# Pattern A's score matmuls: one fp32 product becomes two fp32r products of split operands

## The chip, the cores and the metric

One Trainium2 chip, and the kernel runs on one of its cores. The metric is the device time of one execution in microseconds. "Before" was run three times, beside one execution under the profiler.

## What is computed

A two-layer encoder trunk. In each layer the normalised input (512 tokens, 1024 features) goes through one wide projection, four attention patterns read parts of it, each pattern's output is projected, gated and summed, and an MLP follows. The change is in pattern A, a windowed attention with 8 query heads on 2 key/value heads:

```python
def windowed_gqa(a_q, a_k, a_v, pos, q_norm, k_norm, sink):
    q = rms_norm(a_q.reshape(b, s, A_KV_HEADS, grp, HEAD_DIM), q_norm)   # 8 heads of 64
    k = rms_norm(a_k.reshape(b, s, A_KV_HEADS, HEAD_DIM), k_norm)        # 2 heads of 64
    ...
    o, _ = banded_attention(q, k, v, pos, A_RADIUS, slopes, sink)        # |i - j| <= 128
# banded_attention: s = q.k / sqrt(d) - slope*|pos_i - pos_j|, masked outside the band,
# softmax with the sink logit in the denominator, then p.v
```

## The kernel before

**Two sorts of matmul.** The projections use split operands: a float32 value x is stored as a high part (x rounded to the type fp32r) and a low part (x minus the high part, also fp32r), and a product is three fp32r matmuls, high by high, low by high, high by low (`split3`; the matmuls all carry line L565). Weights arrive in `s_raw`, ACT writes the high part `s_wh` (L937), DVE the low part `s_wl` (L1413). The attention's transposes (L594), its values (L787) and its scores (L797, for pattern B L841) are matmuls of plain float32 operands instead. The profile has two LDWEIGHTS and two MATMUL instructions for each float32 score or value matmul, and one of each for a fp32r one.

**An order written out by hand.** A layer is 752 steps; a step is the six L565 matmuls of two chunks for one of the four output banks. `ORDER` lays the projections on the steps. Every other piece of work is a generator that yields the step at which it is due (`yield at`), and `together` merges the generators of an engine by due time into its one instruction stream, which the engine then runs strictly in that order, each instruction behind its semaphore waits. So a wait on an engine holds all that stands behind it. A weight tile's split (L937, L1413) is due 7.6 steps before the tile's first use, if its buffer is free.

**Attention.** `WINDOW` gives each pattern its stretch of steps; pattern A has steps 312 to 376 and 32 units (one head of one tile of 128 queries each, 8 heads for a tile) on 36 slots, one slot each 1.78 steps. In a slot PE transposes the probabilities of unit u-2 (L594), multiplies those of unit u-3 with the values (L787), and makes the scores of unit u into the bank S1 (L797). A unit has 256 key columns in tiles 0 and 3 and 384 in tiles 1 and 2 (`near_keys`). PE makes the scores of unit u only after `s_biased` of unit u-1: DVE adds the bias to S1 (L1918), ACT takes the exponential (L1236, L1241), ACT and DVE each copy half of the transposes (L1229, L1854).

**The queries of A.** `qA` has two heads in the two halves of the partitions. ACT copies them to `q_pad` [128, 4, 2, 128], where a head stands in its own 64 partitions and the other 64 are zero, so that one matmul over 128 partitions with `kA` (both halves hold the same key head) gives that head's scores. `tiles_of` does this in 8 pieces of two copies (L1270), four heads of one tile in a piece; a piece is due almost a whole piece of units ahead of its first unit, except the first two, which are due half a step before slot 0. PE waits for `q_padded` before a unit's scores. `kA` is written by ACT at L1182 behind the "kv" projection, in four turns; in the same turns ACT and DVE write the latent's high (L1185) and low (L1795) parts, and PE's next turn waits for them on `td_act` and `td_dve`.

Of the kernel before, what the change touches and what calls it, by code (L numbers as in the profile page):

```python
# [13 lines left out]
F32 = mybir.dt.float32  # L14
# [92 lines left out]
class Own:  # L107
# [13 lines left out]
    nt_dve=24, ta_ready=128, ta_act=128, ta_dve=128, q_padded=64, s_ready=144, s_biased=144, p_ready=144, b_mixed=16, o_ready=128, o_out=24,  # L121
    gains_in=1, ssum=16, lam_dot=1, lam_exp=1, c_diff=2, c_exp=2, merged_sum=24, merged_hi=8, merged_lo=8, conv_mid=44,
    e_ready=22, hidden_val=22, hidden_hi=22, hidden_lo=22, act_step=189, dve_step=513, params_in=16, direct_in=8,
# [41 lines left out]
PADS = dict(C0=16, C1=8, C2=8, A=16, B=16)  # L165


def pads_of(name, u):

    return u + 1 if PADS[name] == 8 else 4 * (u // 8) + 2 * (u % 8 // 4) + 2  # L170

# [53 lines left out]
def _build(nc, io, ctx):  # L225
# [23 lines left out]
    AD = 7168  # L249
    work = sb("work", [P, AD + 15872])  # L250
# [31 lines left out]
    kA, vA = in_work(AD + 14336, 1024, g=2), in_work(AD + 15360, 512, t=4)  # L282
# [54 lines left out]
    q_padded = signal("q_padded")  # L337
    s_ready = signal("s_ready")
# [191 lines left out]
    def _(pe):  # L530
# [3 lines left out]
        def layer(l):  # L534
# [227 lines left out]
            def attention(name, scores_of, values_of, per_out, begun, keys=all_keys, tile_of=None):  # L762
# [6 lines left out]
                for step, at, pace in slots(name):  # L769
# [19 lines left out]
                    if step < n:  # L789
                        if step == 0:  # L790
                            for handle, count in begun:
                                pe.wait_ge(handle, count)
                        if name in PADS:
                            pe.wait_ge(*q_padded.at(l, pads + pads_of(name, step)))
                        pe.wait_ge(*s_biased.at(l, first + step))
                        for out, st, mv in scores_of(step, S1):
                            last = mm(out, st, mv, start=True, stop=True)  # L797
                        last.then_inc(*s_ready.up())
# [9 lines left out]
            def attention_b(scores_of, begun):  # L808
# [5 lines left out]
                for step, at, pace in slots("B"):  # L814
# [19 lines left out]
                    if step < n:  # L834
                        if step == 0:
                            for handle, count in begun:
                                pe.wait_ge(handle, count)
                        pe.wait_ge(*q_padded.at(l, n_pad[0] + pads_of("B", step)))
                        pe.wait_ge(*s_biased.at(l, first + step))
                        for out, st, mv in scores_of(step, S1):  # L840
                            mm(out, st, mv, start=True, stop=True).then_inc(*s_ready.up())  # L841
# [11 lines left out]
            def attentions():  # L853

                def near_scores(k_of):
                    def scores_of(u, out):
                        lo, hi, _mid = near_keys(u)
                        h = u % 8
                        return [(out[:, P * lo:P * hi], q_pad[:, h // 2, h % 2, :], k_of(h)[:, P * lo:P * hi])]
                    return scores_of  # L860

                def residue_scores(j):
                    return lambda h, out: [(out[:, P * r:P * r + P], q_pad[:, r, h % 2, :],
                                            CK[j][:, h // 2, P * r:P * r + P]) for r in range(RES)]
# [5 lines left out]
                def b_scores(u, out):  # L870
                    n = 4 * (u % 2) + (u % 8) // 2
                    return [(out[:], q_pad[:, n // 2, n % 2, :], kT[:, n // 2, :])]
# [7 lines left out]
                for j in (1, 2):  # L880
                    yield from attention(f"C{j}", residue_scores(j), residue_values(j), 2, heads_in(8 * j + 9, 12 * j + 12))
                yield from attention("D", lambda u, out: [(out[:], qD[0:DQK, u % 8, P * (u // 8):P * (u // 8) + P], kD[0:DQK, u % 8, :])],
                                     token_values(lambda u, k: vD[u % 8 // 4][:, k, DV * (u % 4):DV * (u % 4) + DV], DV, 8), 8,
                                     heads_in(53, 68), tile_of=out_tiles)
# [11 lines left out]
    def _(act):  # L896
# [47 lines left out]
        def layer(l):  # L944
# [304 lines left out]
            def pads():  # L1249
# [21 lines left out]

                def residues_of(j, turns_done):
# [18 lines left out]
                yield from tiles_of("A", qA, 57, by_pair)  # L1291
# [60 lines left out]
    def _(dve):  # L1352
# [62 lines left out]
        def layer(l):  # L1415
# [356 lines left out]
            def turns():  # L1772
# [189 lines left out]
            return norm1(), dense(), turns(), attentions(), c_combine()  # L1962
# [31 lines left out]
```

## Time and profile before

| | |
|---|---|
| three runs | 2741.24, 2744.35, 2745.07 us; median 2744.35 us |
| the profiled execution | 2741.32 us; its span, first to last instruction, 2739.5 us |
| mean granted TensorE clock | 0.996 of full speed |
| busy | PE 97%, weight loads 81%, DVE 57%, ACT 45% of the span |

The span is what the trace shows; 1.8 us of the profiled execution lie around it. The profile names the engines PE (matmuls), PEld (their weight loads), DVE (VectorE), ACT (ScalarE) and SP (SyncE). L and a number is a line of the kernel. A tile's name is that of its memory: `s_work` holds nearly all the attention tiles. The trace calls the type of fp32r matmul operands f32; an L565 matmul is fp32r.

### The profile page before, as it was taken

What the parts mean: (1) busy time and instruction counts of PE and PEld (TensorE: products, weight loads), DVE (VectorE), ACT (ScalarE), POOL (GpSimd) and SP (SyncE); (2) the same over time, 40 slices, a digit from 0 to 9 for tenths busy, and PEclk for the clock granted to TensorE, in tenths of its full rate; (3) what the DMA queues carried; (4) which work ended last, traced back from release to release, by engine and by line L of the source; (5) the groups of instructions that cost most, each with busy time, mean ns of one, the idle gap of its engine ahead of it and who ended that gap; (6) DMA issues with size and microseconds to landing.
All of it is one profiled execution on the core that took longest, in us unless ns stands there. A gap on an engine that the chain in (4) does not pass through costs nothing. (4 is left out here: it accounts for less than half of the span.)

```text
span 2739.5 us, 35859 instructions
## 1 busy us (share of the span) xinstructions
PE 2644.2 (97%) x12974; PEld 2215.0 (81%) x12974; DVE 1565.9 (57%) x3276; ACT 1232.0 (45%) x2510; POOL 1.5 (0%) x6
## 2 busy tenths in 40 slices
PE   5999999999999989999999999999999999899999
PEld 4899987777877778888879998877788777788887
DVE  5564577544566556464764546775455566464645
ACT  5455555444544334242454555544445443342423
POOL 0000000000000000000000000000000000000000
PEclk9999999999999999999999999999999999999999
DMA  5212223222121323333342122221222213232333
GB/s 167 77 55 78 81 63 92 62 65 82 55 72 52 101 86 92 100 93 100 93 123 70 47 86 74 80 83 54 70 78 68 63 47 108 85 100 93 99 93 100
DMA packets 143872, 225.26 MB, mean 82 GB/s; under 512 B 15046, under 2 KB 69458, under 8 KB 142802
## 3 DMA queue, kind: packets, MB, share of 16 engines
q1 hardware_dynamic: 135842, 201.85, 24.7%
q10 hardware_dynamic: 7856, 21.12, 2.1%
q8 instruction: 106, 1.74, 0.3%
q14 instruction: 68, 0.56, 0.1%
HBM read 210.29 MB, written 12.65 MB: 81 GB/s over the span
## 5 line engine op out<-in xcount | busy, mean ns | idle before, releaser
L1413 DVE TENSOR_TENSOR s_wl<-s_raw,s_wh 128x1024 fp32r<-128x1024 f32 (+2 forms) x376 | 453.7, 1207 | 382.0 <-ACT s_wh L937 380.6
L937 ACT ACTIVATE s_wh<-s_raw 128x1024 fp32r<-128x1024 f32 (+2 forms) x376 | 392.3, 1043 | 440.8 <-PE bank L565 423.3
L565 PE MATMUL bank<-s_hTh,s_wh 128*128 128x512 f32 x1216 | 520.4, 428 | 3.6 <-DVE s_hTl L1517 3.6
L565 PE MATMUL bank<-s_hTh,s_wl 128*128 128x512 f32 x1216 | 474.7, 390 | 0.0
L565 PE MATMUL bank<-s_hTl,s_wh 128*128 128x512 f32 x1216 | 473.9, 390 | 0.0
L565 PE MATMUL bank<-s_wh,s_hTh 128*128 128x512 f32 (+1 forms) x1088 | 469.6, 432 | 3.5 <-DVE s_early L1530 3.3
L565 PE MATMUL bank<-s_wh,s_hTl 128*128 128x512 f32 (+1 forms) x1088 | 426.0, 392 | 0.0
L565 PE MATMUL bank<-s_wl,s_hTh 128*128 128x512 f32 (+1 forms) x1088 | 425.4, 391 | 0.0
L565 PEld LDWEIGHTS bank<-s_hTh,s_wh 128*128 128x128 f32 x1216 | 228.6, 188 | 70.9 <-issue 27.3
L1241 ACT ACTIVATE s_work<-s_work,s_stat 128x128 f32<-128x128 f32 (+3 forms) x320 | 167.5, 524 | 257.7 <-DVE s_work L1929 113.5
L565 PEld LDWEIGHTS bank<-s_hTl,s_wh 128*128 128x128 f32 x1216 | 228.8, 188 | 66.6 <-issue 24.4
L565 PEld LDWEIGHTS bank<-s_wh,s_hTh 128*128 128x128 f32 x1088 | 251.8, 231 | 37.5 <-issue 3.7
L565 PEld LDWEIGHTS bank<-s_wl,s_hTh 128*128 128x128 f32 x1088 | 253.5, 233 | 27.4 <-issue 0.5
L565 PEld LDWEIGHTS bank<-s_wh,s_hTl 128*128 128x128 f32 x1088 | 251.6, 231 | 26.9
L565 PEld LDWEIGHTS bank<-s_hTh,s_wl 128*128 128x128 f32 x1216 | 228.2, 188 | 49.0
L594 PE MATMUL bank<-s_consts,s_work 128*128 128x128 f32 (+1 forms) x1432 | 216.3, 273 | 11.6 <-DVE s_gTl L1770 7.3
L594 PEld LDWEIGHTS bank<-s_consts,s_work 128*128 128x128 f32 (+1 forms) x1432 | 173.1, 139 | 65.0 <-issue 28.2
L1854 DVE COPY s_work<-bank 128x128 f32<-128x128 f32 (+1 forms) x224 | 77.5, 346 | 230.4 <-PE bank L594 111.8
L565 PE MATMUL bank<-s_wh,s_gTh 128*128 128x512 f32 (+1 forms) x432 | 167.6, 388 | 5.3 <-ACT s_work L965 5.3
L565 PE MATMUL bank<-s_wh,s_gTl 128*128 128x512 f32 (+1 forms) x432 | 166.9, 386 | 0.0
L565 PE MATMUL bank<-s_wl,s_gTh 128*128 128x512 f32 (+1 forms) x432 | 166.8, 386 | 0.0
L1229 ACT ACTIVATE s_work<-bank 128x256 f32<-128x256 f32 (+1 forms) x224 | 78.4, 350 | 92.8 <-PE bank L594 91.3
(189 smaller groups left out, 3376.9 us busy)
## 6 DMA issues: line engine op xcount, KB each, us to landing
s_raw<-in_w_in SPq DMA_DIRECT2D x168, 512.0 KB, 3.6
s_raw<-in_ffn_w_up SPq DMA_DIRECT2D x176, 256.0 KB, 3.1
s_raw<-in_ffn_w_down SPq DMA_DIRECT2D x44, 512.0 KB, 3.7
s_raw<-in_w_branch SPq DMA_DIRECT2D x32, 512.0 KB, 3.7
s_raw<-in_w_o SPq DMA_DIRECT2D x16, 512.0 KB, 3.7
x_keep<-s_work ACTq DMA_DIRECT2D x2, 2048.0 KB, 6.9
s_raw<-in_w_in SPq DMA_DIRECT2D x16, 256.0 KB, 2.9
gate_keep<-s_early ACTq DMA_DIRECT2D x4, 1024.0 KB, 4.3
```

Of the source, the lines that this page charges most:

```text
L565: last = mm(PJ[b][:, 0:width], st, mv, start=i == 0 and n == 1, stop=i == ntiles - 1 and n == 3 * chunks)
L594: last = nc.tensor.transpose(dst[0:m, (at + n) * P:(at + n) * P + k], src, ident[0:k, 0:k])
L937: a(wh[:, k % 3, 0:n], raw[:, s, 0:n], ACT.Copy).then_inc(*hi_split.up(own))
L1229: a(probsT[:, u % 2, P * lo:P * mid], src[:, P * lo:P * mid], ACT.Copy).then_inc(*ta_act.up(own))
L1241: a(probs[:, u % 2, x0:x0 + w], scores[:, u % 2, x0:x0 + w], ACT.Exp, scale=-1.0, bias=stat[:, mins, c:c + 1], accum_out=stat[:, sums, c:c ...
L1413: v.tensor_tensor(wl[:, k % 3, 0:n], raw[:, k % 2, 0:n], wh[:, k % 3, 0:n].bitcast(F32), ALU.subtract).then_inc(*tile_split.up(own))
L1854: v.tensor_copy(probsT[:, u % 2, P * mid:P * hi], src[:, P * mid:P * hi]).then_inc(*ta_dve.up(own))
```

## The change

- `kA` becomes fp32r. ACT writes the high part in all 128 partitions as before (L1182), and DVE then overwrites partitions 64 to 127 with the low part: four new DVE instructions a layer, one in each turn of "kv", ahead of L1795's.
- The queries of A go to `q_two` [128, 4 pairs, 2 halves, 2 sets, 128], fp32r, in a part of `s_work` that pattern D's keys leave free. Set 0 is the head's high part, in both halves of the partitions; set 1 is its low part in partitions 0 to 63 and zero below.
- ACT writes the high part once (16 copies of 64x256 a layer, in place of the 16 to `q_pad`) and, ahead of the first piece, the zeros (two copies of 64x512). DVE writes the second copy of the high part from the first, across the partitions, and subtracts to make the low part: two instructions for each of ACT's 16, in a new stream `stacks()` due 0.1 step behind ACT's.
- PE makes a unit's scores with two fp32r matmuls that accumulate: set 0 with `kA` (high query by high key, plus high query by low key in the other half) and set 1 with `kA` (low query by high key). It waits for `q_stacked` in place of `q_padded`, and at slot 0 also for `q_zeroed`.
- All other lines of the diff only pass `start` and `stop` along.

```diff
-PADS = dict(C0=16, C1=8, C2=8, A=16, B=16)
+PADS = dict(C0=16, C1=8, C2=8, B=16)
...
+    kA, vA = stacked[:, AD + 14336:AD + 15360].rearrange("p (g n) -> p g n", g=2), in_work(AD + 15360, 512, t=4)
+    q_two = stacked[:, AD + 4096:AD + 6144].rearrange("p (c h s n) -> p c h s n", c=4, h=2, s=2)
...
+                        if name == "A":
+                            pe.wait_ge(*q_stacked.at(l, pads_of(name, step)))
...
+                def stacked_scores(u, out):
+                    lo, hi, _mid = near_keys(u)
+                    h = u % 8
+                    return [(out[:, P * lo:P * hi], q_two[:, h // 2, h % 2, s, :],
+                             kA[:, h // 4, P * lo:P * hi], s == 0, s == 1) for s in range(2)]
...
-                yield from attention("A", near_scores(lambda h: kA[:, h // 4, :]),
+                yield from attention("A", stacked_scores,
...
-                                     heads_in(57, 72), keys=near_keys, tile_of=out_tiles)
+                                     heads_in(57, 72) + [q_zeroed.at(l, 2)], keys=near_keys, tile_of=out_tiles)
...
+                def stacks_of_a():
+                    first, slot = done, slots("A")
+                    for piece in range(8):
+                        t, g = piece // 2, piece % 2
+                        yield slot[4 * piece - 4][1] + 0.8 * slot[0][2] if piece >= 2 else slot[0][1] - 0.5
+                        if piece == 0:
+                            act.wait_ge(*td_dve.at(l, 57))
+                        act.wait_ge(*s_ready.at(l, first + 4 * piece - 4 if piece >= 2 else first))
+                        if piece == 0:
+                            for half in range(2):
+                                act.wait_ge(*own.done(l))
+                                a(q_two[64:128, :, half, 1, :], q_pad[64:128, :, 0, :], ACT.Copy).then_inc(*q_zeroed.up(own))
+                        for half in range(2):
+                            mine = slice(64 * half, 64 * half + 64)
+                            act.wait_ge(*own.done(l))
+                            a(q_two[mine, 2 * g:2 * g + 2, half, 0, :], qA[mine, 2 * g:2 * g + 2, P * t:P * t + P],
+                              ACT.Copy).then_inc(*q_hi.up(own))
...
                 for t in range(4):
                     yield END["kv"] + 6.8 + 2 * t
                     src = group()
+                    key = kA[64:128, :, P * t:P * t + P]
+                    dve.wait_ge(*own.done(l))
+                    v.scalar_tensor_tensor(key, src[64:128, 0:256].rearrange("p (c n) -> p c n", c=2), prm[64:128, ROW["ak"]:ROW["ak"] + 1],
+                                           key.bitcast(F32), ALU.mult, ALU.subtract).then_inc(*dve_step.up(own))
...
+            def stacks():
+
+                slot, n = slots("A"), 0
+                for piece in range(8):
+                    t, g = piece // 2, piece % 2
+                    yield (slot[4 * piece - 4][1] + 0.8 * slot[0][2] if piece >= 2 else slot[0][1] - 0.5) + 0.1
+                    for half in range(2):
+                        n += 1
+                        mine, other = slice(64 * half, 64 * half + 64), slice(64 - 64 * half, 128 - 64 * half)
+                        dve.wait_ge(*q_hi.at(l, n))
+                        dve.wait_ge(*own.done(l))
+                        v.tensor_copy(q_two[other, 2 * g:2 * g + 2, half, 0, :], q_two[mine, 2 * g:2 * g + 2, half, 0, :].bitcast(F32)).then_inc(*dve_step.up(own))
+                        dve.wait_ge(*own.done(l))
+                        v.tensor_tensor(q_two[0:64, 2 * g:2 * g + 2, half, 1, :], qA[mine, 2 * g:2 * g + 2, P * t:P * t + P],
+                                        q_two[mine, 2 * g:2 * g + 2, half, 0, :].bitcast(F32), ALU.subtract).then_inc(*q_stacked.up(own))
...
-            return norm1(), dense(), turns(), attentions(), c_combine()
+            return norm1(), dense(), turns(), stacks(), attentions(), c_combine()
```

## Rows read from the trace of the kernel before

**Rows 1.** The page's first part: busy time, share, instructions by engine.

```profile
PE 2644.2 (97%) x12974; PEld 2215.0 (81%) x12974; DVE 1565.9 (57%) x3276; ACT 1232.0 (45%) x2510; POOL 1.5 (0%) x6
```

**Rows 2.** Windows over pattern A, layer 0: us, busy by engine, clock, DMA share, GB/s.

```profile
653.00:715.00 62.00, 61.27 (x317) 50.16 (x316) 32.74 (x75) 29.67 (x80) 0.00 (x0) 1.00 0.26 77
715.00:777.00 62.00, 60.89 (x338) 50.94 (x336) 40.77 (x109) 36.34 (x99) 0.00 (x0) 1.00 0.25 75
```

**Rows 3.** PE's waits: total us, times, longest.

```profile
PE bank L797 <- DVE s_stat L1918: 1.5, 2, 0.7
...
PE bank L594 <- DVE s_gTl L1795: 1.0, 2, 0.5
```

**Rows 4.** Timeline, a 256-column unit: start us, us, engine, line, operands, idle before.

```profile
661.79 0.56 PE L787 MATMUL bank<-s_work 128*128 128x64 f32 x4
...
662.18 0.65 PE L797 MATMUL bank<-s_work,s_q_pad 128*128 128x256 f32 x2
...
662.48 0.58 PE L565 MATMUL bank<-s_gTh,s_wh 128*128 128x512 f32 x1
```

**Rows 5.** Timeline, a 384-column unit.

```profile
701.03 0.78 PE L787 MATMUL bank<-s_work 128*128 128x64 f32 x6
...
701.65 0.86 PE L797 MATMUL bank<-s_work,s_q_pad 128*128 128x384 f32 x2
```

**Rows 6.** Timeline, fp32r matmuls of 384 columns: first and eleventh in a row.

```profile
402.00 0.33 PE L565 MATMUL bank<-s_wh,s_gTh 128*128 128x384 f32 x1
...
403.75 0.33 PE L565 MATMUL bank<-s_wl,s_gTh 128*128 128x384 f32 x1
```

**Rows 7.** Groups by shape, ACT and DVE: busy us, mean ns of one, idle before.

```profile
L1284 ACT ACTIVATE s_q_pad<-s_work 64x512 f32<-64x512 f32 x16 | 10.1, 630 | 1.5
...
L1369 DVE CAST s_work<-s_work 128x512 f32<-128x512 int32 x1 | 0.4, 427 | 0.0
...
L1548 DVE TENSOR_TENSOR s_work<-s_work,s_trig 128x256 f32<-128x256 f32 x4 | 1.7, 426 | 0.1
...
L1505 DVE SCALAR_TENSOR_TENSOR s_hTl<-bank,s_prm,s_hTh 128x256 fp32r<-128x256 f32 x32 | 15.3, 483 | 14.4 <-ACT s_hTh L1027 13.1
```

**Rows 8.** Timeline, slots 0 and 1 of pattern A in layer 0.

```profile
651.35 1.82 ACT L1270 ACTIVATE s_q_pad<-s_work 64x256 f32<-64x256 f32 x4
...
653.16 0.59 PE L797 MATMUL bank<-s_work,s_q_pad 128*128 128x256 f32 x2
...
653.98 0.48 DVE L1918 CUSTOM_DVE_ANT_0 s_work<-bank,s_near,s_sink 128x256 f32<-128x256 f32 x1 [3.42 <-PE bank L797]
...
654.98 0.59 PE L797 MATMUL bank<-s_work,s_q_pad 128*128 128x256 f32 x2
```

**Rows 9.** Timeline, piece 2 of the queries and what follows it.

```profile
670.11 0.86 ACT L1270 ACTIVATE s_q_pad<-s_work 64x256 f32<-64x256 f32 x2
...
671.36 0.29 DVE L1854 COPY s_work<-bank 128x128 f32<-128x128 f32 x1 [1.79 <-ACT s_work L1229]
...
672.70 0.48 DVE L1918 CUSTOM_DVE_ANT_0 s_work<-bank,s_near,s_sink 128x256 f32<-128x256 f32 x1
...
673.33 0.67 PE L797 MATMUL bank<-s_work,s_q_pad 128*128 128x256 f32 x2 [0.73 <-DVE s_stat L1918]
```

**Rows 10.** Timeline, piece 4 of the queries and DVE's next instruction.

```profile
700.28 0.86 ACT L1270 ACTIVATE s_q_pad<-s_work 64x256 f32<-64x256 f32 x2
...
701.70 0.29 DVE L1854 COPY s_work<-bank 128x128 f32<-128x128 f32 x1 [2.44 <-PE bank L594]
```

**Rows 11.** Timeline, the first two turns of "kv" and PE's next turns.

```profile
365.39 0.74 DVE L1795 SCALAR_TENSOR_TENSOR s_gTl<-bank,s_prm,s_gTh 128x128 fp32r<-128x128 f32 x2
...
366.28 1.06 PE L594 MATMUL bank<-s_consts,s_work 128*128 128x128 f32 x8
...
370.12 0.74 DVE L1795 SCALAR_TENSOR_TENSOR s_gTl<-bank,s_prm,s_gTh 128x128 fp32r<-128x128 f32 x2 [1.84 <-ACT s_gTh L1185]
...
371.00 0.63 PE L594 MATMUL bank<-s_consts,s_work 128*128 128x128 f32 x4 [0.49 <-DVE s_gTl L1795]
```

More of the change, by code:

```diff
@@ L120 @@
     pj_dve=108, sq_used=60, normed=53, combined=4, sublayer_normed=4, h_normed=5, h_scaled=3, rstd=3, td_ready=77, td_act=77, td_dve=77, nt_ready=16, nt_act=24,
[L121 removed]
+    nt_dve=24, ta_ready=128, ta_act=128, ta_dve=128, q_padded=48, q_hi=16, q_stacked=16, q_zeroed=2, s_ready=144, s_biased=144, p_ready=144, b_mixed=16, o_ready=128, o_out=24,
     gains_in=1, ssum=16, lam_dot=1, lam_exp=1, c_diff=2, c_exp=2, merged_sum=24, merged_hi=8, merged_lo=8, conv_mid=44,
[L123 removed]
+    e_ready=22, hidden_val=22, hidden_hi=22, hidden_lo=22, act_step=189, dve_step=533, params_in=16, direct_in=8,
     x_moved=2, c0_moved=6, gates_moved=4,
@@ L249, in _build @@
     AD = 7168
+    with nc.sbuf_tensor("s_stacked", [P, AD + 15872], F32R) as stacked:
+        pass
     work = sb("work", [P, AD + 15872])
@@ L337, in _build @@
     q_padded = signal("q_padded")
+    q_hi = signal("q_hi")
+    q_stacked = signal("q_stacked")
+    q_zeroed = signal("q_zeroed")
     s_ready = signal("s_ready")
@@ L794, in attention @@
                             pe.wait_ge(*q_padded.at(l, pads + pads_of(name, step)))
+                        if name == "A":
+                            pe.wait_ge(*q_stacked.at(l, pads_of(name, step)))
                         pe.wait_ge(*s_biased.at(l, first + step))
-                        for out, st, mv in scores_of(step, S1):
-                            last = mm(out, st, mv, start=True, stop=True)
+                        for out, st, mv, start, stop in scores_of(step, S1):
+                            last = mm(out, st, mv, start=start, stop=stop)
                         last.then_inc(*s_ready.up())
@@ L839, in attention_b @@
                         pe.wait_ge(*s_biased.at(l, first + step))
-                        for out, st, mv in scores_of(step, S1):
-                            mm(out, st, mv, start=True, stop=True).then_inc(*s_ready.up())
+                        for out, st, mv, start, stop in scores_of(step, S1):
+                            mm(out, st, mv, start=start, stop=stop).then_inc(*s_ready.up())
             def token_values(v_of, width, places, keys=all_keys):
@@ L858, in scores_of @@
                         h = u % 8
-                        return [(out[:, P * lo:P * hi], q_pad[:, h // 2, h % 2, :], k_of(h)[:, P * lo:P * hi])]
+                        return [(out[:, P * lo:P * hi], q_pad[:, h // 2, h % 2, :], k_of(h)[:, P * lo:P * hi], True, True)]
                     return scores_of
+                def stacked_scores(u, out):
[3 more added lines that the diff above has]
+                             kA[:, h // 4, P * lo:P * hi], s == 0, s == 1) for s in range(2)]
                 def residue_scores(j):
                     return lambda h, out: [(out[:, P * r:P * r + P], q_pad[:, r, h % 2, :],
-                                            CK[j][:, h // 2, P * r:P * r + P]) for r in range(RES)]
+                                            CK[j][:, h // 2, P * r:P * r + P], True, True) for r in range(RES)]
                 def residue_values(j):
@@ L871, in b_scores @@
                     n = 4 * (u % 2) + (u % 8) // 2
-                    return [(out[:], q_pad[:, n // 2, n % 2, :], kT[:, n // 2, :])]
+                    return [(out[:], q_pad[:, n // 2, n % 2, :], kT[:, n // 2, :], True, True)]
                 def heads_in(turns_done, evacuated):
@@ L1290, in pads @@
                 done += WINDOW["D"][2]
-                yield from tiles_of("A", qA, 57, by_pair)
+                yield from stacks_of_a()
+                done += WINDOW["A"][2]
                 yield from tiles_of("B", qT, B_HEADS, by_map)
```

5 lines of the change are left out of this document (2 added, 3 removed).

## The prediction

> **What bounds the kernel now.** I read the page's busy line first: PE is busy 97% of the span, DVE 57%, ACT 45% [rows 1]. Busy PE is not PE at its peak, so I next cut out pattern A's window. Its 124 us in layer 0 have 122.2 us of PE at full granted clock, 73.5 us of DVE and 66.0 us of ACT [rows 2]. So PE sets the time there, and a matmul that gets shorter should shorten the kernel, unless PE then waits for another engine. PE's waits say how near that is: once in each layer it waits 0.7 us for DVE's bias before a score, and once in each layer 0.5 us for the low part of the latent in a turn of "kv" [rows 3]. Both places matter below, since the change puts more work on DVE right before them.
>
> **What the scores cost PE now.** Busy times of pipelined matmuls overlap, so I take ends. At a 256-column unit the values end at 661.79+0.56 = 662.35 and the two score instructions at 662.18+0.65 = 662.83: 0.48 us. The next L565 ends at 663.06, 0.23 later, its usual pitch, so nothing of the unit hides beyond its own end [rows 4]. At 384 columns the same difference is 702.51-701.81 = 0.70 us [rows 5]. The 128 columns more cost 0.22 us, 1.7 ns a column: four streams of the columns at 2.4 GHz (0.42 ns each), with about 0.055 us left over that do not grow with the columns.
>
> **What they will cost.** Fp32r streams the columns once. Eleven fp32r matmuls of 384 columns start 1.75 us apart over ten steps, 0.175 each [rows 6]; with 512 columns the pitch is 0.23 [rows 4]. That is 0.42 ns a column and about 15 ns fixed, so 0.121 us at 256 columns, a width for which the trace has no fp32r row. Two of them and the same 0.055 left over: 0.30 us at 256, 0.405 at 384. A unit saves 0.18 or 0.30 us. There are 32 units of each width in the two layers: 5.8 + 9.6 = **15.4 us saved**. Bounds: at 256 columns no faster than the 384 row gives 12.2; with nothing left over beside the two streams it is 18.9.
>
> The Trainium skill's page "TensorE: Matmul & The Clock Gate", section "Back-to-back issue gap", puts a matmul at N/2.4 + 2.5 ns, 109 ns at 256 columns and 163 at 384. By it, and with no remainder, the saving would be 20.7 us. The trace disagrees at 384 columns, where it has 175, so I stay with the rows.
>
> **What DVE gets.** In `stacks()` 16 copies and 16 subtractions a layer, each 256 elements on 64 partitions. The subtraction is like L1548, 0.43 us [rows 7]. For a copy from SBUF to SBUF the nearest row is the CAST of 512 elements in 0.43; half the elements should take 0.28 to 0.30, and never more than the 0.43 of the two-source row. I take 0.29, since CAST is also one source with a change of type. Add some 0.035 between two dependent DVE instructions, an estimate from ACT's own four copies in rows 8, pitched 0.47 at 0.42 long. A half is 0.79 us and **a piece of four 1.58 us**. The four low parts of the keys are like L1505, 0.48 [rows 7]. All this is 8 x 1.58 + 4 x 0.52 = 14.7 us of DVE a layer, 12.6 of them in a window with 50 us of DVE idle. It fits as a sum; what counts is where it falls, as DVE runs in a fixed order.
>
> The page "VectorE: DVE Perf Modes", section "Mode 2×_2P — use both read ports for one tensor", lets a one-source fp32 instruction between SBUF operands make two elements a cycle. The CAST row agrees (512 elements in less time than one a cycle at 0.96 GHz would need). If the copies were refused it, at 0.43 a piece would be 1.86 us, and the forecast some 1.6 us later.
>
> **The start of pattern A.** This is the new wait. Now ACT writes four copies from 651.35 in 1.82 us and PE has its first score at 653.16, without a wait [rows 8]. After: ACT first writes two zero copies of 0.63 (L1284's shape [rows 7]), pitched 0.67, to 652.69, then high part one until 653.10 and two until 653.56. DVE copies and subtracts the first from 653.14 to 653.90 and the second from 653.93 to 654.69. PE's `q_stacked` wait is met at about 654.75: 1.6 us late. Nothing hides this, since all of PE's matmuls stand behind the waiting score. DVE then has piece 1, which is due at the same step, until 656.27, and only then L1918 for unit 0 (now at 653.98), done near 656.8. PE reaches score 1 after 1.6 us of dense work, at 656.35, and waits 0.5 more. Behind DVE's blocks also stands the weights' low part L1413, behind ACT's zeros the high part L937 and one gate's evacuation; these come 1.4 to 2 us later, but a tile is split 7.6 steps (over 10 us) before its use, and the evacuated bank is needed only three steps later, so they stay hidden. Loss **2.1 us a layer**, bounds 1.2 (piece 1 finds a gap) and 3.
>
> **Pieces 2 to 7.** Each is written a slot or more ahead of need, so `q_stacked` is never the late one; the question is whom 1.58 us of DVE push back. Piece 2: ACT's copies start at 670.11, so DVE's block runs 670.56 to 672.14 where it was idle for 1.79 us, but L1854 was due at 671.36 and now starts at 672.17; 1.34 us behind it comes L1918, 673.5 in place of 672.70. PE already waits 0.73 us for that one [rows 9]. So PE loses 0.8 more, and of the savings of the slot before 0.2 are only waited away: 1.0 us. Piece 4: copies from 700.28, DVE's block 700.75 to 702.3, L1854 0.6 late from 701.70, DVE idle 2.44 us before it [rows 10], and L1918 waits for PE's score anyway: nothing. Pieces 3, 5, 6 and 7 I followed in the same way: 3 and 6 push L1918 back by 0.3 and 1.4 us, which is done more than a microsecond before PE's next score; 5 and 7 fall in idle DVE time. **1.0 us a layer**, bounds 0.4 and one more piece exposed (2.6).
>
> **"kv".** The low part of the key delays L1795's end by 0.52 us. In the first turn L1795 ends at 366.13 and PE's next turn starts at 366.28; in the second the ends are 370.86 and 371.00, with 0.49 us of wait already [rows 11]. Both pass on nearly all: **0.9 us a layer**, bounds 0.5 and 1.1. Turns three and four have slack.
>
> **What costs nothing.** ACT's 16 copies keep their number and shape. PE's instruction count stays (two loads and two matmuls a unit), as do the waits.
>
> **The sum.** 2 x (2.1 + 1.0 + 0.9) = 8.0 us lost, 15.4 saved: 7.4 us faster. The profiled execution's 2741.32 would become 2733.9. It lies 3.0 us under the median of the three runs, near the lowest of them; carried over to the median, 2744.35 - 7.4 = **2737 us**.
>
> **The rivals.** 0.2% of this kernel, 5.5 us, is about what a measurement can tell from no change.
> - *As forecast*, 4 to 11 us saved: 0.55, of it 0.43 beyond 5.5 us.
> - *The losses are mostly hidden*: DVE catches up at piece 2, and the start costs only its 1.2 us. Then 15.4 - 2 x (1.2 + 0 + 0.5) = 12.0 saved, 2732.4. For it: four tenths of DVE's time in the window are free [rows 2]. Against: the start's chain has no work over it. 0.20.
> - *PE is handed from matmul to DVE*: two more pieces a layer stand ahead of a bias that PE waits for. 2 x 2 x 1.58 = 6.3 more lost, 1.1 saved, 2743.3. For it: shorter scores bring PE to each wait sooner, and the second half of the window has DVE at 66% [rows 2]. Against: the gaps found at pieces 4, 5 and 7. 0.17.
> - *Slower*: every one of the six later pieces lands ahead of a bias that PE is waiting for. 2 x (2.1 + 6 x 1.58 + 0.9) = 25.0 lost, 9.6 us slower, 2754. It turns the sign from three pieces a layer fully exposed, and passes 5.5 us at 4.7 of six. Against: rows 10. That fp32r at 256 columns streamed more than once is, I think, excluded by the slope between 384 and 512. 0.08.
>
> **How the numbers follow.** Faster 0.43 + 0.20 = 0.63; same 0.12 + 0.17 = 0.29; slower 0.08. The range from 2730 to 2745 takes in the hidden case with the upper bounds of the saving, and the third case; outside are the slower case and an end of the second. The likeliest case's own range is 2733.5 to 2740.5.
>
> **What would show it.** L797 of pattern A as fp32r ends 0.30 and 0.40 us behind the values (0.48 and 0.70 now). DVE has 36 more instructions a layer; the copies near 0.29. A new PE wait of about 1.6 us at the first score of A, another of 0.5 before the second, 1.5 in place of 0.73 at the score behind piece 2 (673.33), and about 0.5 and 1.0 us in "kv". The prediction is wrong if DVE's copies are twice as long, if pieces 3 or 6 show up as PE waits, or if ACT reaches the zeros earlier than 651.35 and takes the start's wait away.

## The result: slower, where 7 us less were forecast

| | median, us | range | runs |
|---|---|---|---|
| before | 2744.27 | 2740.29 to 2746.70 | 20 |
| after | 2748.44 | 2744.83 to 2750.08 | 20 |

The ratio is 1.0016, with a 95% interval of 1.0009 to 1.0023: some 4 us slower, and 3.4 us beyond the upper end of the forecast's range. By the forecast's own bound of 0.2% it counts as no change; the sign is clear all the same. The profiled execution of after took 2744.83 us, its span is 2743.0 against 2739.5, and its mean granted clock 0.994 against 0.996.

The page's first part for after, to lay beside [rows 1]: PE has 10.5 us less to do in the same 12,974 matmuls, DVE 24.3 us more in 72 more instructions.

```profile
PE 2633.7 (96%) x12974; PEld 2211.1 (81%) x12974; DVE 1590.2 (58%) x3348; ACT 1232.7 (45%) x2514; POOL 1.5 (0%) x6
```

Windows over pattern A of layer 0 after (columns as in [rows 2]). PE was busy 122.2 of 124 us; now it is busy 115.3 of 122.0, so about 6.7 us stand open. DVE went from 73.5 us of 124 to 82.9 of 122.

```profile
656.00:718.00 62.00, 58.30 (x318) 49.36 (x319) 39.48 (x95) 30.42 (x83) 0.00 (x0) 1.00 0.26 77
718.00:778.00 60.00, 56.95 (x334) 49.05 (x333) 43.46 (x119) 35.26 (x98) 0.00 (x0) 1.00 0.25 75
```

In after's numbering PE's transposes are L600, its values L793 and its scores L805; the bias is L1971, the halves of the transposes' copies L1243 (ACT) and L1907 (DVE), a tile's output L2000 to L2004. PE's waits of after in the same window (total us, times, longest). Before, the same view has two rows: 0.7 us for the bias, and 1.1 us of L787 for the tile output of L1951.

```profile
PE bank L793 <- DVE s_work L2004: 2.1, 2, 1.5
PE bank L805 <- DVE s_stacked L1886: 1.6, 1, 1.6
PE bank L600 <- DVE s_work L1907: 1.3, 2, 0.9
PE bank L793 <- ACT s_work L1243: 1.1, 1, 1.1
PE bank L805 <- DVE s_stat L1971: 1.1, 2, 0.9
```

**Where the time went.** Both kernels issue the same matmuls in the same order, so I set the profiles side by side matmul by matmul and noted where the difference of their end times, after minus before, jumps by 0.3 us or more. Layer 0:

```
place (time before -> after)               step, us
kv turn 2                 366.28 -> 366.69   +0.53
kv turn 3                 371.00 -> 371.93   +0.52
turn of the next projection
                          391.36 -> 392.81   +0.52
first score of A          653.16 -> 657.09   +1.82
second score                                 +0.27
transposes at piece 2     671.80 -> 676.21   +0.86
values behind piece 3     691.76 -> 695.72   +0.83
values behind tile 1      725.99 -> 728.02   +0.39
transposes at piece 6     739.86 -> 741.52   +0.58
values behind piece 7     761.25 -> 763.03   +1.28
between these, a unit of A          -0.2 or -0.3 each
```

Layer 1 has the same places, with 1.64 at the last. In the window of A the saving wins by 1.25 us in layer 0 and 0.9 in layer 1; "kv" and the turn behind it take 1.57 a layer back. That leaves after some 1.0 us behind. The rest of the 3.5 us between the two profiles comes in two places, in each of which PE runs at half its clock for 3.4 us longer than before: the difference grows by 0.6 us between 410 and 427, and by 2.0 us between 1010 and 1025.

**The saving is there.** Timeline of after, PE, a unit of 256 columns and one of 384 (columns as in [rows 4]). The ends lie 666.51 - 666.23 = 0.28 and 692.04 - 691.63 = 0.41 us apart, 0.48 and 0.70 before.

```profile
665.67 0.56 PE L793 MATMUL bank<-s_work 128*128 128x64 f32 x4
666.03 0.48 PE L805 MATMUL bank<-s_stacked 128*128 128x256 f32 x2
...
691.07 0.56 PE L793 MATMUL bank<-s_work 128*128 128x64 f32 x4
691.44 0.60 PE L805 MATMUL bank<-s_stacked 128*128 128x384 f32 x2
```

Over all units the trace's finer times give 0.291 and 0.403, against 0.488 and 0.701: 32 x 0.197 + 32 x 0.298 = 15.8 us saved. The second matmul of a pair takes 118 ns at 256 columns and 174 at 384. The Trainium skill's page "TensorE: Matmul & The Clock Gate", section "Back-to-back issue gap", would have 109 and 163; the trace lies 9 to 11 ns above them. The remainder that does not grow with the columns stays 55 ns (0.291 less two times 0.118).

**The start of A**, timeline of after. ACT's four copies come behind the zeros, from 654.80; DVE's two halves for piece 0 end at 656.84, and PE waits 1.62 us. DVE then has piece 1's two before the bias at 658.56, for which PE waits 0.27.

```profile
655.25 0.29 DVE L1884 CAST s_stacked<-s_stacked 64x256 fp32r<-64x256 f32 x1 [2.55 <-ACT s_stacked L1301]
655.57 0.42 DVE L1886 TENSOR_TENSOR s_stacked<-s_work,s_stacked 64x256 fp32r<-64x256 f32 x1
...
657.09 0.47 PE L805 MATMUL bank<-s_stacked 128*128 128x256 f32 x2 [1.62 <-DVE s_stacked L1886]
...
658.56 0.48 DVE L1971 CUSTOM_DVE_ANT_0 s_work<-bank,s_near,s_sink 128x256 f32<-128x256 f32 x1
...
659.20 0.48 PE L805 MATMUL bank<-s_stacked 128*128 128x256 f32 x2 [0.27 <-DVE s_stat L1971]
```

**Piece 2**, the counterpart of [rows 9]. DVE's block pushes its half of the transposes' copies (L1907) back, and PE now waits 0.89 us at the next transposes and 0.86 at the score.

```profile
674.28 0.29 DVE L1884 CAST s_stacked<-s_stacked 64x256 fp32r<-64x256 f32 x1 [0.99 <-ACT s_stacked L1301]
...
675.79 0.28 DVE L1907 COPY s_work<-bank 128x128 f32<-128x128 f32 x1
...
676.21 0.41 PE L600 MATMUL bank<-s_consts,s_work 128*128 128x128 f32 x2 [0.89 <-DVE s_work L1907]
...
677.87 0.47 PE L805 MATMUL bank<-s_stacked 128*128 128x256 f32 x2 [0.86 <-DVE s_stat L1971]
```

**Behind piece 3**: DVE from the end of the piece to the tile output. The bias of 690.52 is soon enough, as forecast. But DVE then works for 5 us with no gap over 0.2 us, and piece 3's 1.7 us have pushed back everything up to L2004, the output of tile 0, and that is what PE's next values wait for.

```profile
689.86 0.42 DVE L1886 TENSOR_TENSOR s_stacked<-s_work,s_stacked 64x256 fp32r<-64x256 f32 x1
...
690.52 0.62 DVE L1971 CUSTOM_DVE_ANT_0 s_work<-bank,s_near,s_sink 128x384 f32<-128x384 f32 x1
...
691.06 0.68 DVE L1563 SCALAR_TENSOR_TENSOR s_work<-s_work,bank 128x512 f32<-128x512 f32 x1
...
692.38 1.22 DVE L1446 TENSOR_TENSOR s_wl<-s_raw,s_wh 128x1024 fp32r<-128x1024 f32 x1
...
693.52 0.28 DVE L1907 COPY s_work<-bank 128x128 f32<-128x128 f32 x1
...
693.72 0.61 DVE L1971 CUSTOM_DVE_ANT_0 s_work<-bank,s_near,s_sink 128x384 f32<-128x384 f32 x1
...
694.88 0.69 DVE L2004 TENSOR_TENSOR s_work<-bank,s_stat 128x512 f32<-128x512 f32 x1
```

**"kv"**, the counterpart of [rows 11], and the turn of the projection behind it, whose low part (L1838) ends DVE's chain.

```profile
366.69 1.06 PE L600 MATMUL bank<-s_consts,s_work 128*128 128x128 f32 x8 [0.68 <-DVE s_gTl L1832]
...
371.93 0.63 PE L600 MATMUL bank<-s_consts,s_work 128*128 128x128 f32 x4 [1.00 <-DVE s_gTl L1832]
...
392.81 0.52 PE L600 MATMUL bank<-s_consts,s_work 128*128 128x128 f32 x3 [0.60 <-DVE s_gTl L1838]
```

**DVE's new instructions**, groups by shape. The durations are as forecast; a half takes 0.84 us from start to start, a piece of four 1.68.

```profile
L1886 DVE TENSOR_TENSOR s_stacked<-s_work,s_stacked 64x256 fp32r<-64x256 f32 x32 | 13.4, 419 | 1.1
L1884 DVE CAST s_stacked<-s_stacked 64x256 fp32r<-64x256 f32 x32 | 9.2, 288 | 17.0 <-ACT s_stacked L1301 14.7
L1828 DVE SCALAR_TENSOR_TENSOR s_stacked<-bank,s_prm,s_stacked 64x256 fp32r<-64x256 f32 x8 | 3.9, 491 | 9.2 <-ACT s_gTh L1199 9.0
```

### The profile page after: what moved, and what is told of

It reads as the page before. It is cut to its first block and busy times, and to the rows that moved or that the text cites. A ratio compares the mean times of both kernels' runs of the same rounds, so it can differ in the third digit from the quotient of the medians.

```text
span 2743.0 us, 35969 instructions
## 1 busy us (share of the span) xinstructions
PE 2633.7 (96%) x12974; PEld 2211.1 (81%) x12974; DVE 1590.2 (58%) x3348; ACT 1232.7 (45%) x2514; POOL 1.5 (0%) x6
## 5 line engine op out<-in xcount | busy, mean ns | idle before, releaser
L571 PE MATMUL bank<-s_wh,s_hTh 128*128 128x512 f32 (+1 forms) x1088 | 457.4, 420 | 3.6 <-DVE s_early L1563 3.3
L600 PE MATMUL bank<-s_consts,s_work 128*128 128x128 f32 (+1 forms) x1432 | 216.3, 273 | 16.9 <-DVE s_gTl L1803 6.8
L600 PEld LDWEIGHTS bank<-s_consts,s_work 128*128 128x128 f32 (+1 forms) x1432 | 173.1, 139 | 70.9 <-issue 33.7
L1907 DVE COPY s_work<-bank 128x128 f32<-128x128 f32 (+1 forms) x224 | 77.3, 345 | 204.4 <-PE bank L600 96.5
L1243 ACT ACTIVATE s_work<-bank 128x256 f32<-128x256 f32 (+1 forms) x224 | 78.0, 348 | 85.9 <-PE bank L600 84.7
```

The costliest lines, as they stand in the source:

```text
L571: last = mm(PJ[b][:, 0:width], st, mv, start=i == 0 and n == 1, stop=i == ntiles - 1 and n == 3 * chunks)
L600: last = nc.tensor.transpose(dst[0:m, (at + n) * P:(at + n) * P + k], src, ident[0:k, 0:k])
L1243: a(probsT[:, u % 2, P * lo:P * mid], src[:, P * lo:P * mid], ACT.Copy).then_inc(*ta_act.up(own))
L1907: v.tensor_copy(probsT[:, u % 2, P * mid:P * hi], src[:, P * mid:P * hi]).then_inc(*ta_dve.up(own))
```

## The experiments

Twelve kernels were measured in three sets, each set beside its own runs of the kernel before (median 2743.20, 2743.37 and 2743.49 us). "To before" is the difference of medians. The mean clock is TensorE's granted clock, 1 being full speed. All but `keycost` start from the kernel after.

| kernel | median, us | runs | to before | ratio, 95% | mean clock |
|---|---|---|---|---|---|
| again | 2748.29 | 11 | +4.9 | 1.0009 to 1.0026 | 0.9929 |
| nostack | 2733.08 | 5 | -10.1 | 0.9950 to 0.9975 | 0.9942 |
| nokey | 2741.87 | 11 | -1.3 | 0.9986 to 1.0004 | 0.9943 |
| early | 2742.31 | 11 | -0.9 | 0.9992 to 1.0010 | 0.9935 |
| actcopy | 2754.41 | 5 | +11.2 | 1.0026 to 1.0051 | 0.9920 |
| matmulonly | 2729.38 | 5 | -14.0 | 0.9941 to 0.9966 | 0.9948 |
| halves | 2742.99 | 11 | -0.4 | 0.9991 to 1.0009 | 0.9939 |
| placed | 2742.70 | 11 | -0.7 | 0.9989 to 1.0007 | 0.9936 |
| nocopy | 2739.07 | 11 | -4.4 | 0.9974 to 0.9991 | 0.9939 |
| pool | 2735.00 | 6 | -8.5 | 0.9959 to 0.9982 | 0.9935 |
| poolkv | 2732.69 | 5 | -10.8 | 0.9948 to 0.9973 | 0.9940 |
| keycost | 2747.99 | 11 | +4.5 | 1.0008 to 1.0026 | 0.9943 |

The kernel before has a mean clock of 0.9945 to 0.9947 over the 70 runs beside them. The intervals reach some 2.4 us to either side with 11 runs and 3.4 us with 5 or 6, so differences under 3.5 us between two of these rows are not read.

**nostack: the scores without DVE's stacks.** Both score matmuls read ACT's high part; DVE's copies and subtractions are gone, the keys' low parts stay.

```diff
-            return norm1(), dense(), turns(), stacks(), attentions(), c_combine()
+            return norm1(), dense(), turns(), attentions(), c_combine()
...
-                            a(q_two[mine, 2 * g:2 * g + 2, half, 0, :], qA[mine, 2 * g:2 * g + 2, P * t:P * t + P],
+                            a(q_two[:, 2 * g:2 * g + 2, half, 0, :], qA[:, 2 * g:2 * g + 2, P * t:P * t + P],
```

> The changed kernel without DVE's stream of copies and subtractions: ACT writes the high parts of both heads over all 128 partitions (same count and length of ACT copies), both score matmuls use set 0, and PE waits for ACT alone. Left out: the queries' low parts and the separation of the two heads. PE's two fp32r matmuls, the zeros and the keys' low part stay. Theory 1 (DVE's blocks stand ahead of DVE work for which PE waits; by lining up the two profiles matmul by matmul they cost 12.4 us, the saving 15.8): some 11 us below the changed kernel, 2737. Theory 2 (the saving is lost to a lower granted clock and not to DVE's blocks): within 3 us of the changed kernel, above 2745. Theory 3 (the fp32r matmuls save less than the pitch says): not below 2741.

Measured -10.1 us to before, 2733, where the first theory said 2737. It is the one that fits: the other two needed 2741 or more. The 64 instructions of the stacks cost 15 us in the kernel after, nearly all of the saving, though their 22.6 busy us have 100 us of idle DVE time in the two windows. Of the 15 us, the higher clock (0.9942 for 0.9929 in `again`) makes up to 3.6.

**nokey: without the keys' low part.**

```diff
-                    v.scalar_tensor_tensor(key, src[64:128, 0:256].rearrange("p (c n) -> p c n", c=2), prm[64:128, ROW["ak"]:ROW["ak"] + 1],
-                                           key.bitcast(F32), ALU.mult, ALU.subtract).then_inc(*dve_step.up(own))
```

> The changed kernel without the four DVE instructions a layer that write the keys' low part (left out: that part; the lower half of the keys keeps the high part). Theory 1: PE's turns of kv and of cq come 1.45 us a layer earlier, so 2.9 us below the changed kernel, about 2745.5. A rival, that these waits are absorbed by later ones: no difference.

Measured 6.2 us less than `again`, each against its own before, twice what was expected. The forecast gave these eight instructions 1.8 us; 2 x 1.57 = 3.1 are the waits seen above, and the clock (0.9943 for 0.9929) is worth up to 3.8.

**early: pieces 0 and 1 six steps sooner**, on ACT and DVE, nothing else changed.

```diff
-                        yield slot[4 * piece - 4][1] + 0.8 * slot[0][2] if piece >= 2 else slot[0][1] - 0.5
+                        yield slot[4 * piece - 4][1] + 0.8 * slot[0][2] if piece >= 2 else slot[0][1] - 6.5
```

> The changed kernel with the zeros and pieces 0 and 1 due six steps earlier, at step 305.5 on ACT and 305.6 on DVE, behind the last scores of pattern D. Theory 1: PE's wait before the first scores of A goes (1.8 and 0.3 us in each layer), so 4.2 us below the changed kernel, about 2744.3. Rival: DVE's block now falls before D's tile outputs and PE waits there instead: no gain.

Measured 5.8 us less than `again`, against twice the forecast start of 2.1 = 4.2; the clock (0.9935 for 0.9929) is worth up to 1.6. PE's waits in its window (640 to 780): those of the start are gone, all others stand, and one of 0.3 us is new.

```profile
PE bank L793 <- DVE s_work L2004: 2.1, 2, 1.5
PE bank L600 <- DVE s_work L1907: 1.3, 2, 0.9
PE bank L793 <- ACT s_work L1243: 1.2, 1, 1.2
PE bank L805 <- DVE s_stat L1971: 0.9, 1, 0.9
PE bank L793 <- DVE s_work L1907: 0.3, 1, 0.3
```

**actcopy: ACT makes the second copy instead of DVE.**

```diff
                             a(q_two[mine, 2 * g:2 * g + 2, half, 0, :], qA[mine, 2 * g:2 * g + 2, P * t:P * t + P],
+                              ACT.Copy).then_inc(*act_step.up(own))
+                            other = slice(64 - 64 * half, 128 - 64 * half)
+                            act.wait_ge(*own.done(l))
+                            a(q_two[other, 2 * g:2 * g + 2, half, 0, :], qA[mine, 2 * g:2 * g + 2, P * t:P * t + P],
                               ACT.Copy).then_inc(*q_hi.up(own))
...
-                        v.tensor_copy(q_two[other, 2 * g:2 * g + 2, half, 0, :], q_two[mine, 2 * g:2 * g + 2, half, 0, :].bitcast(F32)).then_inc(*dve_step.up(own))
```

> The changed kernel with ACT writing both copies of the high half (32 ACT copies a layer for 16), DVE only the subtraction. DVE's piece falls from 1.68 to about 0.9 us, ACT's grows from 0.9 to 1.8. Theory 1: pieces 2 to 7 cost half of 8.2 us, the start costs the same or 0.3 more a layer: 3 to 4 us below the changed kernel, about 2745. Theory 4 (in this window ACT is as tight as DVE): no gain or a loss, with new PE waits for ACT's L1243 and for the banks' evacuation.

Measured +11.2 us to before, 6 us worse than the kernel after, where the first theory said 3 to 4 us better; the fourth came true. ACT is 45% busy over the span and has no room here either, since it makes the exponentials and half of the copies that hand PE its probabilities. In the window of A of layer 0, PE's waits sum to 8.8 us in place of 7.2: for ACT's copy (L1243) 1.8 in place of 1.1, and for the tile output 2.5 in place of 2.1, though DVE has less to do. The clock, the lowest of all, is worth up to 2.5 us.

**again and matmulonly: the whole cost of DVE's work in one pair.** `again` is the kernel after unchanged; `matmulonly` is `nostack` and `nokey` together, so PE, ACT's copies and the zeros are all that is left of the change.

> The changed kernel as it is, for its time and granted clock beside the others on one chip. Every theory: ratio 1.0016 to before, about 2748; by the amended theory 1 a mean granted clock about 0.001 under that of before (0.9931 to 0.9945 so far), worth some 3 us, and about 1 us of waits over savings.

> The changed kernel without DVE's stacks and without the keys' low part (both left out, as in the two runs before): only PE's two fp32r matmuls in place of the fp32 one, with ACT's zeros. Theory 1: the whole saving of 15.8 us less some 1.2 us for ACT's zeros at the start of A: 14.6 below before, about 2729, with the clock of before (0.9945). Theory 3 (the fp32r matmuls save less): above 2733.

`matmulonly` is 14.0 us under before, which fits the forecast's 15.4 for the matmuls (ACT's zeros still cost a wait of 0.45 us a layer). Matmul by matmul, `again` minus `matmulonly` in layer 0:

```
kv and the projection behind it    0.52  0.54  0.54
start of A                         1.20  0.50
transposes and score at piece 2    0.95
values at tile output 0 (piece 3)  0.72
values behind tile 1               0.24
transposes at piece 6              0.61
values behind piece 7              1.04
```

Layer 1 has the same steps (1.37 behind piece 7). Together 6.9 and 7.2 us of waits. The two kernels are 18.9 us apart; the clock, 0.9948 and 0.9929 of the span, makes up to 5.2 of it. The two, 14.1 and 5.2, add up to the difference within 0.4.

**halves and placed: the pieces spread out.** `halves` is `early` with every piece from the third on cut in two, a slot apart, and due 0.4 of a slot behind its slot's start in place of 0.8. `placed` also gives "kv"'s turns 2.5 steps in place of 2, on PE, ACT and DVE.

```diff
+                            if half and piece >= 2:
+                                yield slot[4 * piece - 4 + 1][1] + 0.4 * slot[0][2]
...
-                    yield END["kv"] + 6.8 + 2 * t
+                    yield END["kv"] + 6.8 + 2.5 * t
```

> The changed kernel with pieces 0 and 1 six steps early (as in the run early) and each later piece in two halves, due in two neighbouring slots and in the middle of the slot (0.4) where it was 0.8. All of DVE's work stays. Theory 1 (what costs is where DVE's blocks stand): the eight us of pieces 2 to 7 fall to two or three, so 4.2 + 5 us below the changed kernel, about 2739. Rival (what costs is the sum of DVE's work): as the run early, 2742 to 2744.

> As halves, and the four turns of kv 2.5 steps apart on PE, ACT and DVE where they were 2. Theory 1: PE's three waits of 0.5 us a layer behind the keys' low parts go as well, 3 us below halves, about 2736, with the clock of before. Rival: the later turns push on those of cq and on DVE's rsqrt, no gain over halves.

Both missed: neither differs from `early`. Matmul by matmul, `halves` gains 0.6 us at piece 2 and 0.6 at piece 6 and loses 0.9 at 688 and 0.95 around 692, where the half-pieces of piece 3 now stand before the transposes' copies and the tile output. The waits move and keep their sum, 5.9 us in the window for the 5.8 of `early`. So it is not the length of one block alone that costs: wherever it was put, the same DVE work met another instruction that PE waits for.

**nocopy: the subtraction alone.** ACT writes the high part to all 128 partitions in one instruction, and DVE's copy is gone, so half of the stack holds other data.

```diff
-                        v.tensor_copy(q_two[other, 2 * g:2 * g + 2, half, 0, :], q_two[mine, 2 * g:2 * g + 2, half, 0, :].bitcast(F32)).then_inc(*dve_step.up(own))
```

> The changed kernel without DVE's second copy of the high half: ACT's copies run over 128 partitions in the same time, so set 0 holds both heads (left out: their separation), DVE only subtracts, a block of 0.42 us for one of 0.79. Theory 1: of the 12.4 us that DVE's stacks cost, the start keeps the part of one subtraction (0.9 us of 2.1 a layer is left with ACT's zeros) and pieces 2 to 7 halve: 5 to 7 us under the changed kernel in waits and 2 in granted clock, about 2740. Rival: the copies are cheap and the subtraction costs alike: above 2745.

Measured 9.3 us less than `again`, as expected (2739 for about 2740). Up to 2.7 us of it is the clock's (0.9939 for 0.9929). The 32 copies, 9.2 us of DVE time, cost about what they last, and the 32 subtractions (`nocopy` against `nostack`) 5.7 us for 13.4.

**pool and poolkv: the stacks on GpSimd.** Nothing is left out: GpSimd, idle before, makes the copies and subtractions, ACT's first two pieces are six steps early, and DVE keeps only the keys. `poolkv` adds the 2.5 steps of "kv".

```diff
+                    pool.wait_ge(*q_hi.at(l, n))
+                    nc.gpsimd.tensor_copy(q_two[other, 2 * g:2 * g + 2, half, 0, :], q_two[mine, 2 * g:2 * g + 2, half, 0, :].bitcast(F32)).then_inc(*q_copied.up())
+                    pool.wait_ge(*q_copied.at(0, 16 * l + n))
+                    nc.gpsimd.tensor_tensor(q_two[0:64, 2 * g:2 * g + 2, half, 1, :], qA[mine, 2 * g:2 * g + 2, P * t:P * t + P],
+                                            q_two[mine, 2 * g:2 * g + 2, half, 0, :].bitcast(F32), ALU.subtract).then_inc(*q_stacked.up())
...
-            return norm1(), dense(), turns(), stacks(), attentions(), c_combine()
+            return norm1(), dense(), turns(), attentions(), c_combine()
```

> The whole change with DVE's stacks given to the idle GpSimd: the second copy and the subtraction there, nothing left out, pieces 0 and 1 six steps early as in the run early. Theory 1: DVE's 16 blocks are gone and the pieces have over 10 us of slack, so as nostack (2733.1) or 1 us less, with DVE unchanged but for the keys: 2732 to 2734, ratio 0.996. Rival (GpSimd is slow, or takes SBUF from DVE): PE waits for q_stacked at each piece, or DVE's subtractions grow longer than 1.22 us, above 2738.

> As pool, with the four turns of kv 2.5 steps apart where they were 2. Theory 1: PE's waits behind the keys' low parts (1.45 us a layer) go too, as they did between matmulonly and nostack (3.7 us): 2729 to 2731. Rival: as between placed and halves, no difference.

`pool` is 8.5 us under before, 1 us short of what was expected, and `poolkv` 10.8, the fastest kernel of the case that computes everything: 0.4% under before and 0.6% under after. Its 2.3 us under `pool` are too few to be told from nothing; in its trace the first of PE's two waits in "kv" that `pool` shows, 1.0 us, is still there, and the other, 0.6 us at the next projection, is gone. Beside `early` (-0.9), which has the same early start, GpSimd is worth 7.6 us. Groups by shape of `pool`: an instruction takes 1.7 times as long as on DVE in the mean.

```profile
L544 POOL TENSOR_TENSOR s_stacked<-s_work,s_stacked 64x256 fp32r<-64x256 f32 x32 | 23.4, 733 | 2.6
L542 POOL CAST s_stacked<-s_stacked 64x256 fp32r<-64x256 f32 x32 | 15.5, 483 | 2059.9 <-ACT s_stacked L1314 2058.9
```

The 483 ns are a mean of two sorts. A copy alone takes 0.39 us, and 28 of the 32 do. The other four run beside one of DVE's weight splits (L1459, a subtraction of 128x1024), and take 1.28 us twice and 0.94 twice; the split of the first sort takes 1.31 in place of 1.22.

```profile
674.45 0.39 POOL L542 CAST s_stacked<-s_stacked 64x256 fp32r<-64x256 f32 x1 [23.13 <-ACT s_stacked L1314]
...
675.43 1.31 DVE L1459 TENSOR_TENSOR s_wl<-s_raw,s_wh 128x1024 fp32r<-128x1024 f32 x1
...
675.71 1.28 POOL L542 CAST s_stacked<-s_stacked 64x256 fp32r<-64x256 f32 x1
```

It costs nothing here, because a piece is ready long before its first score. PE's waits of `pool` in the window of A; L806 is the values, L818 the scores, L613 the transposes.

```profile
PE bank L806 <- DVE s_work L2001: 1.7, 2, 1.4
PE bank L818 <- DVE s_stat L1968: 0.8, 1, 0.8
PE bank L613 <- DVE s_work L1904: 0.2, 1, 0.2
```

They sum to 2.7 us, against 7.2 in the kernel after, and none of them is for the stacks.

**keycost: the keys' low part alone, put on the kernel before**, written where nothing reads it.

```diff
+                    v.scalar_tensor_tensor(rows[64:128, 0:2, :], src[64:128, 0:256].rearrange("p (c n) -> p c n", c=2), prm[64:128, ROW["ak"]:ROW["ak"] + 1],
+                                           key, ALU.mult, ALU.subtract).then_inc(*dve_step.up(own))
```

> The kernel before with only the keys' low part added: the four DVE instructions of kv, of the same shape and in the same place, writing to a free tile that nobody reads. Theory 1: PE waits 1.45 us more a layer, 2.9 us in all at full clock, and if the clock's share belongs to these waits another 1 to 3 us: 2746 to 2749, mean granted clock 0.9935. If the clock's share belongs to pattern A: 2746, clock 0.9945.

Measured +4.5 us (2.2 to 7.1 by the interval), as expected, for eight instructions of 0.49 us, 3.9 us of DVE time in all: at this place a microsecond of DVE costs about a microsecond of kernel. Matmul by matmul, five of the six turns in question (all but the first of layer 0) come 0.5 to 0.6 us later. The clock (0.9943 for 0.9946) adds up to 0.9.

## Why the prediction was wrong

- **"15.4 us saved"**: 15.8. The rows gave 0.30 and 0.405 for a unit's scores, measured 0.291 and 0.403. Right. (With the printed 0.70 - 0.405 unrounded, the sum comes to 15.2.)
- **"What DVE gets"**: copies 0.288 (forecast 0.29), subtractions 0.419 (0.43), keys 0.491 (0.48). Right. A piece lasts 1.68 (1.58), because the gap between two dependent instructions, put at 0.035, is 0.065; the ACT copies named for it are 0.47 apart at 0.42 long, which gives 0.05.
- **"The start, 2.1 us a layer"**: the ends fall back by 1.82 and 0.27. Right in size and place; `early` removes it.
- **"Pieces 2 to 7, 1.0 us a layer"**: this is the step that failed. Measured 0.86 + 0.83 + 0.39 + 0.58 + 1.28 = 3.9 us in layer 0 and 4.3 in layer 1, beyond the stated bound of 2.6, and the forecast's own sign of being wrong, "if pieces 3 or 6 show up as PE waits", came up. Piece 2 came as forecast (0.86 for "0.8 more"). For the others I followed DVE's block to one reader only, the bias (L1918 before), found it done "more than a microsecond before PE's next score", and stopped. But DVE's order is fixed, so a block pushes everything behind it until DVE has an idle moment: the output of the tile (L2000 to L2004, for which PE's values wait), the transposes' copies (L1907) and, through ACT, the probabilities (L1243). Piece 3's bias was on time, and the output of tile 0, 4 us later, was not. "5 and 7 fall in idle DVE time" is wrong for 7; behind 5 DVE did idle, and the 0.39 there are added to a wait of 1.1 us that stood before.
- **"kv, 0.9 us a layer"**: 1.57. The first two turns cost 0.53 and 0.51, near the upper bound of 1.1. "Turns three and four have slack" was true of PE's waits and not of DVE: its chain arrives 0.52 us late at the next projection's turn, where PE waits for L1838.
- **The granted clock was no term of the sum.** It fell from a mean of 0.9945 to about 0.993 (`again`). The span times what is missing of the full clock is 15 us before and 19 after: up to 4 us, as an estimate from these rows. In the profiles, the stretches at half clock last 26.5 us before and 33.8 after, which is worth 3.7 us.

The sum redone with the measured terms: 2 x (2.1 + 4.1 + 1.57) = 15.5 us of waits for 15.8 saved, 0.3 us faster. Read off the two profiles side by side it is 1.0 us slower (3.1 in "kv", less the 1.25 and 0.9 won in A), because steps under 0.3 us are not in the sum. So waits and saving cancel to within a microsecond, and which is the larger stays open. Most of the measured 4 us goes with the lower clock: 2.6 of the 3.5 us between the profiles.

Of the rivals the third, "PE is handed from matmul to DVE" (2743.3, given 0.17), comes nearest. Its waits cost 2 x 3.1 us over the forecast's pieces, and the measured surplus is 2 x 3.1. That the numbers agree is chance: it has two more whole pieces ahead of a bias, and what PE waited for was mostly the tile output, the transposes' copies and the probabilities. The runs lie some 5 us above its price: 1.3 of it "kv", the rest about the clock's.

A stretch at half clock behind two waits is seen in `again`, which has one more such stretch inside A than the profile of after. Its timeline behind piece 2 of layer 1: PE has waited 0.88 and 0.86 us within two units, and a microsecond later the matmuls of 512 columns start 0.43 us apart in place of 0.23 (1.2 GHz in place of 2.4), until 2038.9.

```profile
2032.79 0.41 PE L600 MATMUL bank<-s_consts,s_work 128*128 128x128 f32 x2 [0.88 <-DVE s_work L1907]
...
2034.45 0.48 PE L805 MATMUL bank<-s_stacked 128*128 128x256 f32 x2 [0.86 <-DVE s_stat L1971]
...
2034.77 0.40 PE L571 MATMUL bank<-s_gTh,s_wh 128*128 128x512 f32 x1
...
2035.00 0.39 PE L571 MATMUL bank<-s_gTl,s_wh 128*128 128x512 f32 x1
...
2035.88 0.63 PE L571 MATMUL bank<-s_gTl,s_wh 128*128 128x512 f32 x1
...
2036.31 0.63 PE L571 MATMUL bank<-s_gTh,s_wl 128*128 128x512 f32 x1
```

The profile of after has the same two waits at the same place, and its matmuls behind them keep their 0.23 us:

```profile
2032.70 0.41 PE L600 MATMUL bank<-s_consts,s_work 128*128 128x128 f32 x2 [0.88 <-DVE s_work L1907]
...
2034.36 0.47 PE L805 MATMUL bank<-s_stacked 128*128 128x256 f32 x2 [0.86 <-DVE s_stat L1971]
...
2036.06 0.39 PE L571 MATMUL bank<-s_gTh,s_wh 128*128 128x512 f32 x1
...
2036.29 0.39 PE L571 MATMUL bank<-s_gTl,s_wh 128*128 128x512 f32 x1
```

Windows of `again` there and around 1010, where each profile has such a stretch (the seventh number is the clock).

```profile
1008.00:1020.00 12.00, 5.33 (x24) 4.33 (x22) 7.61 (x21) 5.52 (x12) 0.00 (x0) 0.79 0.28 86
2034.00:2040.00 6.00, 5.54 (x22) 4.59 (x23) 1.13 (x6) 3.07 (x9) 0.00 (x0) 0.72 0.31 87
```

What stays open is the clock's share. Such stretches inside A stand in the profiles of `again`, `placed` and `nocopy` (one each) and of `actcopy` (two a layer, lowest clock and longest time of all), and in none of before; that the waits bring them is argued from this and not shown. Which wait goes with which stretch can't be told: the profile of after has none inside A, and taking away the keys (0.9943) or the stacks (0.9942) each gives back a part of the clock, the two together more than what was lost. And `pool`, with 2.7 us of waits in the window, has the mean clock of `early`, with 5.8 (0.9935 both). Within the kernel before, a run's time also follows its clock less than fully, by 0.6 to 0.7 us for each one computed, with clocks read to three digits. The 4 us are therefore an upper estimate, and 2 to 4 us is what I would hold to. No run has the waits of after at the clock of before.

## What to carry to other kernels

When you add work to an engine that runs in a fixed order, follow the delay through every instruction behind it until the engine has an idle moment longer than the delay, and for each of them ask who waits, on every engine; the nearest reader being on time proves nothing. An engine at 60% in a window can still be the one that hands PE its next operand in unit after unit; work that can be made well ahead belongs on an engine which no one waits for, even if it takes 1.4 to 1.7 times as long there (4.9 us over before became 0.9 under by starting early, and 8.5 under with the work on GpSimd as well). And where PE is near full, count scattered waits at their length and possibly more: here the kernels with more of them mostly had a lower clock too.

## What the runs showed of the hardware

- A copy of 64x256 from fp32 to fp32r between SBUF tiles, across the halves of the partitions, takes 288 ns on DVE and a two-source subtraction of that shape 419. The Trainium skill's page "VectorE: DVE Perf Modes", section "Mode 2×_2P — use both read ports for one tensor", has a one-source instruction between SBUF operands make two results a cycle and a two-source one not. The trace agrees, by 131 ns on 256 elements, for a copy that also changes partitions and type.
- GpSimd takes 0.39 us for the copy and 733 ns for the subtraction. Beside a two-source DVE instruction of 128x1024 the copy took 1.28 or 0.94 us, and the DVE instruction 1.31 for 1.22 in the two cases with the longer copy (`pool`, four cases of 32; the same in `poolkv`).
- Two waits of 0.88 and 0.86 us in a stream at 96% were followed in one execution by 3.4 us at half clock, worth 1.5 us, and in another by none.
